# Differential layers: the rotary sums of the first two chunks move from GpSimd to VectorE, and the second chunk's step moves ahead of one weight split

## The reference, cut to what matters

```
hn  = rms_norm(x, gain)
qkv = hn @ w_in                      # 1024 -> 3072: q 1024, k 1024, v 1024
q, k = rope(q), rope(k)              # per head of 64:
#   x1, x2 = the two halves of the head
#   [x1*cos - x2*sin, x2*cos + x1*sin]
p = softmax(mask(q @ k.T / 8))       # 8 pairs of heads, causal, 256 x 256
o = (p_first - lam * p_second) @ v   # then a norm per head, and w_out
```

## Time and profile before

| | us |
|---|---|
| median of 3 runs (lowest to highest) | 1450.99 (1450.54 to 1452.69) |
| the profiled execution | 1452.92 |
| its span in the trace | 1451.1 |
| TensorE busy | 1394.6 (96%) |
| VectorE busy | 992.5 (68%) |
| ScalarE busy | 795.4 (55%) |
| GpSimd busy | 191.4 (13%) |

### The profile page before, as it was taken

One profiled execution on the slowest core, in us unless ns is written; L12 is line 12 of the kernel. 1 busy time (PEld: TensorE's weight loads), 2 busy tenths in 40 slices (PEclk: granted clock), 3 DMA queues, 4 the chain that ended last, 5 costly groups with the idle time before them and its releaser, 6 DMA issues.

```text
span 1451.1 us, 20409 instructions
## 1 busy us (share of the span) xinstructions
PE 1394.6 (96%) x6857; PEld 1129.9 (78%) x6857; DVE 992.5 (68%) x1879; ACT 795.4 (55%) x1560; POOL 191.4 (13%) x331
## 2 busy tenths in 40 slices
PE   7899999998999999998999999989999999999998
PEld 6787888886887888887878888767778888777556
DVE  6787755558555755568657555588777767689876
ACT  6565554546654554556656454457665455575334
POOL 4200000000110100002000000021029992000000
PEclk9999999999999999999999999999999999999999
DMA  8442655554422755553226555454346555443132
GB/s 283 145 146 87 218 197 179 186 190 157 147 89 87 240 194 174 198 178 131 88 76 228 178 197 188 159 167 139 117 139 230 175 182 194 143 148 120 55 107 96
DMA packets 154243, 230.54 MB, mean 159 GB/s; under 512 B 7496, under 2 KB 103056, under 8 KB 154176
## 3 DMA queue, kind: packets, MB, share of 16 engines
q1 hardware_dynamic: 152208, 224.24, 45.6%
q0 software_dynamic: 1968, 5.43, 1.3%
HBM read 228.60 MB, written 1.05 MB: 158 GB/s over the span
## 4 chain that ended last, share of the span: by engine, by line
PE 85%; DVE 9%; ACT 3%; issue 2%; POOL 1%; DMA 1%; SPq 0%; DVEq 0%; ACTq 0%
PE ps L2007 25%; PE ps L2009 24%; PE ps L2008 24%; DVE w_rest L1315 2%; PE ps L2775 1%; PE ps L2217 1%; ACT w_head L791 1%; PE ps L2158 1%; POOL qkv L743 1%; DVE x L1370 1%; PE ps L2384 1%; PE ps L2671 1%; ACT scr_a L776 1%; PE ps L2027 1%; DMA w_raw<-in_a_w_in_dram 0%
## 5 line engine op out<-in xcount | busy, mean ns | idle before, releaser
L2007 PE MATMUL ps<-w_head,xt_head 128*128 128x512 f32 (+1 forms) x1376 | 546.4, 397 | 18.0 <-DVE w_rest L1315 7.5
L2009 PE MATMUL ps<-w_head,xt_rest 128*128 128x512 f32 (+1 forms) x1376 | 532.8, 387 | 0.0
L2008 PE MATMUL ps<-w_rest,xt_head 128*128 128x512 f32 (+1 forms) x1376 | 531.7, 386 | 0.0
L1315 DVE SCALAR_TENSOR_TENSOR w_rest<-w_raw,gain_t,w_head 128x512 fp32r<-128x512 f32 (+1 forms) x600 | 417.7, 759 | 77.2 <-ACT w_head L791 76.5
L791 ACT ACTIVATE w_head<-w_raw,gain_t 128x512 fp32r<-128x512 f32 (+1 forms) x600 | 374.3, 700 | 141.3 <-PE ps L2009 123.8
L2007 PEld LDWEIGHTS ps<-w_head,xt_head 128*128 128x128 f32 x1376 | 261.6, 190 | 79.6 <-DVE xt_rest L1322 15.8
L2009 PEld LDWEIGHTS ps<-w_head,xt_rest 128*128 128x128 f32 x1376 | 261.3, 190 | 53.4
L2008 PEld LDWEIGHTS ps<-w_rest,xt_head 128*128 128x128 f32 x1376 | 262.1, 190 | 47.0
L1313 DVE TENSOR_TENSOR w_rest<-w_raw,w_head 128x1024 fp32r<-128x1024 f32 x124 | 153.7, 1281 | 85.8 <-ACT w_head L791 85.8
L791 ACT ACTIVATE w_head<-w_raw 128x1024 fp32r<-128x1024 f32 x124 | 124.7, 1054 | 105.2 <-PE ps L2009 94.8
L2007 PE MATMUL ps<-w_head,ht_head 128*128 128x512 f32 x320 | 125.0, 391 | 0.4 <-DVE ht_rest L1894 0.4
(11 more groups left out here) (476 smaller groups left out, 1382.7 us busy)
## 6 DMA issues: line engine op xcount, KB each, us to landing
w_raw<-in_ffn_w_gate_dram SPq DMA_DIRECT2D x88, 512.0 KB, 3.7
w_raw<-in_ffn_w_up_dram SPq DMA_DIRECT2D x88, 512.0 KB, 4.6
w_raw<-in_ffn_w_down_dram SPq DMA_DIRECT2D x88, 512.0 KB, 4.0
w_raw<-in_a_w_in_dram SPq DMA_DIRECT2D x48, 512.0 KB, 4.6
w_raw<-in_b_w_in_dram SPq DMA_DIRECT2D x24, 512.0 KB, 4.6
w_raw<-in_w_in_dram SPq DMA_DIRECT2D x24, 512.0 KB, 4.5
w_raw<-in_a_w_out_dram SPq DMA_DIRECT2D x16, 512.0 KB, 3.9
w_raw<-in_c_w_in_dram SPq DMA_DIRECT2D x10, 512.0 KB, 4.3
```

What stands on the lines that cost most here:

```text
L1315: ins = dve.scalar_tensor_tensor(w_rest[:, s, w], w_raw[:, s, w], by, hd, ALU.mult, ALU.subtract)
L2007: pe.matmul(out_, hd, wh, start=first, stop=False)
L2008: pe.matmul(out_, hd, wr, start=False, stop=False)
L2009: return pe.matmul(out_, rt, wh, start=False, stop=last)
```

## The change

VectorE now adds the sums of the first two chunks itself, right after the three products of each token half, after waiting for its own last product; it raises `rope_added` in GpSimd's place. GpSimd keeps the sums of chunks 2 and 3. And the second chunk step stands at s = 2 rather than s = 3 of VectorE's loop: ahead of the split of unit 5, not behind it. It still waits until unit 3 has been used.

```
             def rope_adds(before):
-                for j in range(4):
+                for j in (2, 3):
                     for m in range(M):
                         w = cols_of(D_ORDER[j])
                         pool.wait_ge(rope_made, before + M * j + m + 1)
...
                         n["rope"] += 1
+                        if j < 2:
+                            dve.wait_ge(rope_made, n["rope"])
+                            dve.tensor_tensor(qkv[:, m, w], qkv[:, m, w], scr_v[:, m, :], ALU.add).then_inc(rope_added, 1)
...
                 for s in range(12):
-                    if s in (1, 3, 5, 7):
+                    if s in (1, 2, 5, 7):
                         chunk_out(s // 2)
```

## The result

The changed kernel takes 1441.63 us (median of 4 runs, 1441.03 to 1442.07), the kernel before 1451.84 beside it on the same chip (4 runs, 1450.54 to 1453.19). The ratio is 0.9932, with a 95% interval of 0.9919 to 0.9944: 9.9 us faster, 8.1 to 11.8. Forecast was 1442.1. The profiled execution took 1441.98, its span is 1440.3 (before 1451.1).

The account below looks back on a forecast made before the run. The prediction took TensorE as the bound, with its waits for GpSimd's rotary sums and the low clock behind them. Gains of 5.5 and 3.4 us in the two differential layers gave 1450.99 - 8.9 = 1442.1 us, range 1439.4 to 1446.0.

Parts of the forecast that it names:

- What bounds: TensorE bounds the kernel; its two waits for GpSimd's rotary sums, 6.4 us together, cost more than their length through low clock.
- The sum on VectorE, 0.71 of path each: Each sum moved to VectorE adds 0.71 us to its path, 1.42 per chunk step, between 0.42 and 1.49.
- The 0.5 for GpSimd's set-up work: Contention of the first layer's two chunk 0 sums with GpSimd's set-up work: 0.5 us for both, ends 0 and 2.2.
- The upper bound of 1.49: Highest cost of one sum on VectorE, taken as GpSimd's own price, 2.97/2.
- rival A: VectorE becomes the bound in its chain to pair 1's mix; a gain of only 3 to 7 us; chance 0.17.
- The chain of VectorE: VectorE runs gapless from chunk step 0 to pair 1's mix; TensorE waits 1.1 us there; layers gain 5.5 and 3.4.
- The move: Chunk step 1 ahead of unit 5's split costs nothing; left behind it, TensorE would wait 1.8 us behind unit 4.
- A wait of 1.1 to 1.4 leaves the clock alone: TensorE's wait for pair 1's mix doesn't lower its clock, judged by one row with a wait of 1.37 us.
- B: The wait turns up elsewhere, as at unit 8's transfer taking 10 us, not 4.5; gain about 1 us; chance 0.07.
- C: GpSimd's remaining sums, chunks 2 and 3, starve beside VectorE: 4 x 4.4 = 17.6 us lost, 1459.7; chance 0.04.
- D: A gain above 11.4 us: both layers' bounds, 6.7 + 4.7, and some low clock elsewhere gone; chance 0.02.
- The sum: Gains of both differential layers added: 5.5 + 3.4 = 8.9 us.

Follow-up runs that it names:

- doubled sums: The changed kernel with an unused product of the same size behind each of VectorE's new sums; 1449.3 us, 0.9990 of the kernel before.
- first chunk only: The changed kernel, but VectorE sums only chunk 0 and GpSimd chunks 1 to 3; 1453.86 us, 1.0007 of the kernel before.
- first layer only: The changed kernel with the change in the first differential layer only, the second as before; 1445.09 us, 0.9955 of the kernel before.
- move alone: The changed kernel with the second chunk step moved to s = 2, but GpSimd making all sums; 1445.17 us, 0.9960 of the kernel before.
- before with a wait: The kernel before, with VectorE waiting for chunk 0's sums after the first chunk step in the second differential layer; 1454.41 us, 1.0022.

## Why the prediction was right, step by step

**What bounds.** TensorE's wait for GpSimd's sums and the low clock behind it: confirmed. The wait is gone, and with it the low clock.

**The sum on VectorE, 0.71 of path each.** A chunk step with its two sums takes 4.34, and 4.31 was forecast for one without contention: the term was right to 0.03 us. The 0.5 for GpSimd's set-up work in the first layer was too much: all eight sums took 691 to 693 ns. The upper bound of 1.49, called GpSimd's own price, was misread: the 2.97 of that pair is 1.75 for a sum that started beside a split, and 1.26. Alone a sum takes 1.29, so rival A's far end was priced too high.

**The chain of VectorE.** 30.8 us from chunk step 0 to the end of the mix of pair 1 (30.46 to 61.27), forecast 31.6. The 0.5 of contention and 0.3 in the blocks' lengths (5.66 for pair 0 holds a short gap and measures 5.50 without it; 8.74 ends with a duration and is 8.64 from start to start) make the difference, and it started 0.2 earlier. So TensorE waits 0.54 there, not 1.1, and the first layer's gain is 6.2, not 5.5. In the second layer the chain is as long as in the first; ScalarE's table load didn't hold up the mix of pair 0. Hence a wait of 0.80 instead of 1.25, and 3.8 rather than 3.4. The mechanism was right in both, the sizes off by a tenth.

**The move.** Forecast: hidden, and worth 1.8 in the first layer. Without it TensorE waited 1.2 there (and then not for the mix), and the median rose by 1.7 for both layers. The transfer of unit 8 and the split of unit 5 were hidden: unit 5 starts at 45.94, forecast 46.19, and neither is among the waits.

**A wait of 1.1 to 1.4 leaves the clock alone.** This step rested on one row and holds less widely than it was put. Waits of 1.37 and 1.25 left the clock at 1.00, and so did two of 1.2 to 1.3 in one layer with doubled sums. One of 1.53 was followed by 0.79. One of 1.23, with 0.54 shortly before, was followed by 0.83, while the same wait of 1.23 with 0.72 shortly before left it at 1.00. So the length of the wait alone doesn't decide here, and what does stays open. In the changed kernel the waits, 0.54 and 0.80, left the clock at 1.00.

**The rivals.** *A*, VectorE as the bound: the slope is real (2.86 us in the second layer alone, and 5.4 in the trace as a whole, for doubled sums), its price was not met. *B*, a hidden transfer: no sign of it. *C*, starving sums: real, and strong enough to undo the whole change (first chunk only, 1.0007). Its price of 4.4 a pair stood without a working and was low: two starved pairs cost 11.8 us there (1453.86 against 1442.08), 5.9 each. C didn't come about since GpSimd's two remaining pairs are followed by PSUM-reading work of VectorE and not by splits; GpSimd's timeline of the changed kernel:

```profile
54.24 2.72 POOL L743 TENSOR_TENSOR qkv<-qkv,scr_v 128x512 f32<-128x512 f32 x2 [16.42 <-DVE qkv L1440]
```

This is the reason that the prediction gave against C, and it held. *D*, a gain above 11.4, didn't happen.

**The sum.** In the traces the two layers bring 6.2 + 3.8 = 10.0, against 8.9, and the 0.6 us at the window layer's entry lie outside the steps. By medians the gain is 10.2 (1451.84 - 1441.63). The forecast of the time came closer than this, since it started from a median, 1450.99, that lies 0.9 under the one measured beside the change.

## What to carry to other kernels

Before an elementwise sum is left to GpSimd, look at what VectorE runs right behind its inputs: beside instructions that read two operands from SBUF, back to back, its time can grow fivefold, beside PSUM-reading ones it keeps its length. If its result is wanted soon, doing it on VectorE at 0.7 us, or letting VectorE wait the 1.3 us for it, is cheaper than the wait that it causes downstream. And when such a wait is removed, ask the same of the next pair and of the next consumer: three of the variants here only moved it.

## What was not expected of the hardware

**A sum on GpSimd that starts just behind the first split of a block, by 0.16 to 0.17 us, waits, as a rule, for the end of the block.** Eight of the ten such sums in the traces did. They took some 6.3 us beside eight (the kernel before and "first layer only" in the second layer, "first chunk only" in both layers of both of its traces), and 3.7 beside four ("move alone", "before with a wait", in the second layer). The Trainium skill (SBUF — State Buffer, "Who interferes with whom") says that the engine that issues first holds the shared access for the whole instruction; one split is 0.7 us, so by it the sum should lose at most about that. The lengths are those of the blocks, and the measurement decides. The other two, the second sums of chunk 1 in "move alone", started at the same distance and got through in 1.72 and 1.73, each holding up the second split by 1.0 us. What decides between the two outcomes stays open; no run here set the distance between the two instructions on purpose. Where the sum started first, by 0.15 us in the second layers of the kernel before and of "first layer only", it kept its length of 1.28, and the split behind it took the delay; there the one that started first went through.

**Even a tiny instruction can be held up.** In "first layer only" an instruction over 128x2 floats took 1.85 us beside a cast on GpSimd, where its neighbours took 0.16. The timeline:

```profile
25.36 1.85 DVE L1427 TENSOR_TENSOR rs_b<-rs_b,half_ms 128x2 f32<-128x2 f32 x1
...
26.03 1.16 POOL L706 CAST masks_r<-sc 128x1152 fp32r<-128x1152 f32 x1
```

It reads two operands from SBUF, as the splits do. By the profile it started ahead of the cast and ended with it (27.21 and 27.19). VectorE's chain then began at 31.23; in the changed kernel, where two of the splits were held up instead (1.87 and 1.50), it began at 30.46. Over all traces it began between 30.29 and 31.61, depending on which of VectorE's instructions met GpSimd's set-up work, and the mix of pair 1 in the first layer moves with it.
